# Twelve chunks of the branch gates multiplied inside the attention loop of the first mixer, with their logits kept in DRAM

## What is computed

```python
u = _rmsnorm(h, norm_mix)
(nq, kc, vc, ksl, vsl, kwn, vwn, ng, sq, sk, sv, ga, gb) = jnp.split(u @ w_in, pts, axis=-1)
...
o_a = _nsa(nq, kc, vc, ksl, vsl, kwn, vwn, ng, ...)      # compressed, selected and windowed attention, 8 heads
o_b = _banded_attention(sq, sk, sv, SWA_WINDOW, sinks)   # window of 128 with sinks, 8 heads
merged = jax.nn.sigmoid(ga) * (o_a @ w_branch_a) + jax.nn.sigmoid(gb) * (o_b @ w_branch_b)
h = h + merged @ w_out
```

## Time and profile before

| | |
|---|---|
| median of three runs | 2995.52 us (2992.05 to 3009.61) |
| the profiled execution | 2989.28 us, span 2987.5 us |
| PE, DVE, ACT, POOL busy in the span | 92%, 65%, 35%, 43% |
| mean granted clock of PE | 0.955 of full |
| attention loop | from 541.2 to 697.2 us |
| gate stage, to its last matmul | from 697.2 to 787.8 us |

### The profile page before, as it was taken

One profiled execution on the slowest core, in us unless ns is written; L12 is line 12 of the kernel. 1 busy time (PEld: TensorE's weight loads), 2 busy tenths in 40 slices (PEclk: granted clock), 3 DMA queues, 4 the chain that ended last, 5 costly groups with the idle time before them and its releaser, 6 DMA issues. The chain is left out here.

```text
span 2987.5 us, 38641 instructions
## 1 busy us (share of the span) xinstructions
PE 2740.0 (92%) x14085; PEld 2295.0 (77%) x14085; DVE 1947.1 (65%) x3130; ACT 1037.2 (35%) x1635; POOL 1283.5 (43%) x607
## 2 busy tenths in 40 slices
PE   7998999778989998979988999998999969999996
PEld 5887877336778887758876789998999958888785
DVE  5444232683454444366555267778999969999998
ACT  4232321453233223222022233334655524444342
POOL 3443442002434443423042356773222247777773
PEclk9999999699999999989798999999999989999998
DMA  5443341002234443322002245557999999999993
GB/s 177 136 152 116 106 151 50 1 1 64 91 99 141 150 131 113 99 84 78 15 1 64 83 133 158 165 171 282 344 341 353 343 306 373 376 370 376 377 374 137
DMA packets 186680, 528.83 MB, mean 177 GB/s; under 512 B 14032, under 2 KB 96336, under 8 KB 166480
## 3 DMA queue, kind: packets, MB, share of 16 engines
q1 hardware_dynamic: 80208, 292.66, 30.4%
q0 software_dynamic: 18432, 134.23, 11.5%
q10 hardware_dynamic: 87936, 100.68, 9.8%
HBM read 475.08 MB, written 52.43 MB: 177 GB/s over the span
## 5 line engine op out<-in xcount | busy, mean ns | idle before, releaser
L344 POOL TENSOR_TENSOR ring_low<-ring,ring_high 128x1024 fp32r<-128x1024 f32 x323 | 795.0, 2464 | 1164.4 <-ACT ring_high L311 1164.4
L395 PE MATMUL ps<-u_high,ring_high 128*128 128x512 f32 (+1 forms) x1824 | 695.9, 382 | 44.5 <-DVE u_low L618 17.4
L396 PE MATMUL ps<-u_low,ring_high 128*128 128x512 f32 (+1 forms) x1824 | 686.9, 377 | 0.0
L397 PE MATMUL ps<-u_high,ring_low 128*128 128x512 f32 (+1 forms) x1824 | 686.3, 376 | 0.0
L311 ACT ACTIVATE ring_high<-ring 128x1024 fp32r<-128x1024 f32 x355 | 374.5, 1055 | 618.4 <-PE ps L397 549.4
L395 PEld LDWEIGHTS ps<-u_high,ring_high 128*128 128x128 f32 x1824 | 345.6, 189 | 111.3 <-issue 40.9
L396 PEld LDWEIGHTS ps<-u_low,ring_high 128*128 128x128 f32 x1824 | 346.1, 190 | 52.5 <-issue 2.0
L397 PEld LDWEIGHTS ps<-u_high,ring_low 128*128 128x128 f32 x1824 | 345.7, 190 | 52.6
L2346 POOL DMA_INDIRECT fetched_rows<-in_peer_uv,fetch_index x128 | 165.1, 1290 | 339.7 <-DVE ps L2366 302.4
L344 POOL TENSOR_TENSOR ring_low_more<-ring,ring_high_more 128x1024 fp32r<-128x1024 f32 x96 | 243.2, 2546 | 32.3 <-ACT ring_high_more L311 31.7
L2901 DVE TENSOR_TENSOR expert_coef_low<-expert_product,expert_coef_high 128x384 fp32r<-128x384 f32 x128 | 214.7, 1677 | 0.1
(11 more groups left out here) (427 smaller groups left out, 4863.4 us busy)
## 6 DMA issues: line engine op xcount, KB each, us to landing
ring<-in_peer_u SPq DMA_DIRECT2D x128, 512.0 KB
ring<-in_peer_uv SPq DMA_DIRECT2D x128, 512.0 KB
ring<-in_ffn_gu SPq DMA_DIRECT2D x88, 512.0 KB
ada_weights<-in_ada_w SPq DMA_DIRECT2D x48, 512.0 KB, 3.8
ring<-in_ffn_down SPq DMA_DIRECT2D x48, 512.0 KB
expert_acts<-kept_acts ACTq DMA_DIRECT2D x128, 192.0 KB, 4.0
expert_weights<-weight_stage ACTq DMA_DIRECT2D x24, 1024.0 KB, 8.9
group_acts<-expert_acts ACTq DMA_DIRECT2D x16, 1536.0 KB
```

Of the source, the lines that this page charges most:

```text
L344: pool.tensor_tensor(k.lows[p], k.ring[:, s], k.highs[p].bitcast(F32), ALU.subtract)\
L395: pe.matmul(out, k.highs[p][:, w], high, start=first, stop=False)
L396: pe.matmul(out, k.highs[p][:, w], low, start=False, stop=False)
L397: last = pe.matmul(out, k.lows[p][:, w], high, start=False, stop=final)
```

## The change

Twelve of the sixteen gate chunks are multiplied in the attention loop by the new class `GatesBeside`. Each of the 48 units gets a quarter of a chunk, six matmuls, between score(n+2) and turn(n). The products gather in bank 7, and both kinds of mix now use bank 6. After every fourth unit ACT copies bank 7 into one of two tiles of `rope_pair` and splits the next chunk; SP stores the tile to the DRAM tensor `gate_logits`; POOL makes the low part of a chunk. The gate stage loads the twelve tiles back in three DMAs of 1 MB, multiplies only the last four chunks, and scales and takes the sigmoid of all sixteen. The rounding of `o_t` moves there from DVE to ACT, ahead of the first sigmoid.

```diff
--- before.py
+++ after.py
@@ -44,6 +44,7 @@
 PROJ = 16
+BESIDE = 12
 VEC = {}
@@ -100,9 +101,9 @@
 def heads_of_streams(dram):
-    names = ["ffn1_gu", "ffn1_down", "w_in", "w_in_gates", "w_branch", "w_out", "ffn2_gu", "ffn2_down",
-             "w_in_2_state", "w_in_2", "w_out_2", "peer_wq"]
-    return [[dram[n][j] for j in range(SLOTS)] for n in names] + \
+    names = [("ffn1_gu", 0), ("ffn1_down", 0), ("w_in", 0), ("w_in_gates", 0), ("w_in_gates", BESIDE), ("w_branch", 0),
+             ("w_out", 0), ("ffn2_gu", 0), ("ffn2_down", 0), ("w_in_2_state", 0), ("w_in_2", 0), ("w_out_2", 0), ("peer_wq", 0)]
+    return [[dram[n][at + j] for j in range(SLOTS)] for n, at in names] + \
            [[dram["peer_u"][at + j] for j in range(SLOTS)] for at in (0, P // 2)] + \
@@ -399,6 +400,23 @@
                 after(j)
+    def multiply_part(self, pe, j, lo, hi):
+        k, p = self.k, j % self.parts
+        bank, out, parts, opens, closes, _ = self.chunks[j][1][0]
+        if lo == 0:
+            pe.wait_ge(k.low_ready[p].sem, k.low_ready[p].at(j // self.parts + 1))
+            pe.wait_ge(k.emptied[bank].sem, k.emptied[bank].at(j))
+        for m in range(lo, hi):
+            tile, high, low = parts[m]
+            w = slice(tile * P, (tile + 1) * P)
+            pe.matmul(out, k.highs[p][:, w], high, start=m == 0, stop=False)
+            pe.matmul(out, k.highs[p][:, w], low, start=False, stop=False)
+            last = pe.matmul(out, k.lows[p][:, w], high, start=False, stop=m == len(parts) - 1)
+        if hi == len(parts):
+            last.then_inc(k.used[p].sem, 1)
     def wait_products(self, eng, i, j):
@@ -890,19 +908,26 @@
         shifted.finish()
-def gate_tiles(k, weights, tiles, dst, moving, source, split):
-    stream = plain_stream(k, weights, tiles, 4, KD, moving)
+def gate_tiles(k, weights, dst, moving, beside, source, split):
+    stream = plain_stream(k, weights, SLOTS, SLOTS, KD, moving)
     rounded = k.tiles_rounded
     with ExitStack() as tmp:
         scaled = Signal(tmp, k.nc, "gates_scaled")
+        loaded = [Signal(tmp, k.nc, f"gate_logits_loaded{b}") for b in range(3)]
+        rescaled = Signal(tmp, k.nc, "gate_logits_scaled")
         with k.nc.Block() as block:
             @block.sync
             def _(sp):
+                beside.wait_stored(sp)
+                for b in range(3):
+                    sp.dma_start(dst[:, 4 * b:4 * (b + 1)], k.dram["gate_logits"][4 * b:4 * (b + 1)].rearrange("t p n -> p t n"))\
+                      .then_inc(loaded[b].sem, 16)
                 stream.load(sp)
@@ -916,22 +941,30 @@
                 def epilogue(i, j):
-                    act.wait_ge(scaled.sem, i * 4 + (j + 1))
-                    act.activation(one(dst, i * 4 + j), k.ps[:, j], ACT.Sigmoid).then_inc(k.emptied[j].sem, 1)
+                    if j == 0:
+                        for n in range(KD):
+                            act.activation(split.high[:, n], source[:, n], ACT.Copy).then_inc(rounded.sem, 1)
+                    else:
+                        for n in range(4 * (j - 1), 4 * j):
+                            act.wait_ge(rescaled.sem, n + 1)
+                            act.activation(dst[:, n], dst[:, n], ACT.Sigmoid)
+                    act.wait_ge(scaled.sem, j + 1)
+                    act.activation(dst[:, BESIDE + j], k.ps[:, j], ACT.Sigmoid).then_inc(k.emptied[j].sem, 1)
                 stream.scalar(act, epilogue)
             @block.vector
             def _(dve):
-                for i in range(stream.iters):
-                    for t in range(4):
-                        stream.wait_products(dve, i, t)
-                        dve.tensor_tensor(k.ps[:, t], k.ps[:, t], k.rs[:], ALU.mult).then_inc(scaled.sem, 1)
-                        n = i * 4 + t
-                        if n < KD:
-                            dve.tensor_copy(split.high[:, n], source[:, n]).then_inc(rounded.sem, 1)
-                            dve.wait_ge(rounded.sem, rounded.at(n + 1))
-                            dve.tensor_tensor(split.low[:, n], source[:, n], split.high[:, n].bitcast(F32), ALU.subtract)
+                for n in range(KD):
+                    dve.wait_ge(rounded.sem, rounded.at(n + 1))
+                    dve.tensor_tensor(split.low[:, n], source[:, n], split.high[:, n].bitcast(F32), ALU.subtract)
+                for t in range(4):
+                    stream.wait_products(dve, 0, t)
+                    dve.tensor_tensor(k.ps[:, t], k.ps[:, t], k.rs[:], ALU.mult).then_inc(scaled.sem, 1)
+                    if t < 3:
+                        dve.wait_ge(loaded[t].sem, 16)
+                        for n in range(4 * t, 4 * (t + 1)):
+                            dve.tensor_tensor(dst[:, n], dst[:, n], k.rs[:], ALU.mult).then_inc(rescaled.sem, 1)
     stream.finish()
@@ -1288,7 +1321,62 @@
 KINDS = 3
-def attend(k, c, proj, vtok, sigm, o):
+class GatesBeside:
+    BANK = 7
+    def __init__(self, k, ctx, units):
+        self.k = k
+        self.per = units // BESIDE
+        parts = [(x, k.u.high[:, x], k.u.low[:, x]) for x in range(KD)]
+        self.stream = Stream(k, 1, [(chunk_of(k.dram["w_in_gates"], BESIDE, j),
+                                     [(self.BANK, k.ps[:, self.BANK], parts, True, True, None)]) for j in range(BESIDE)])
+        self.kept = k.pair
+        self.stored = [Signal(ctx, k.nc, f"gate_logits_stored{b}") for b in range(2)]
+    def load(self, sp):
+        k, stream = self.k, self.stream
+        ahead = SLOTS + 1
+        stream.load_chunk(sp, 0, SLOTS, stream.chunks[SLOTS][0](0))
+        for j in range(BESIDE):
+            n = j + ahead
+            if n < BESIDE:
+                stream.load_chunk(sp, 0, n, stream.chunks[n][0](0))
+            elif n < BESIDE + SLOTS:
+                stream.load_chunk(sp, 1, n - BESIDE, stream.then[n - BESIDE])
+            sp.wait_ge(k.emptied[self.BANK].sem, k.emptied[self.BANK].at(j + 1))
+            sp.dma_start(k.dram["gate_logits"][j], self.kept[:, j % 2]).then_inc(self.stored[j % 2].sem, 16)
+    def multiply(self, pe, n):
+        j, part = n // self.per, n % self.per
+        self.stream.multiply_part(pe, j, KD * part // self.per, KD * (part + 1) // self.per)
+    def first_split(self, act):
+        self.stream.split_high(act, 0, 1)
+    def take(self, act, n):
+        if n % self.per or n == 0:
+            return
+        k, j = self.k, n // self.per - 1
+        self.stream.wait_products(act, 0, j)
+        if j >= 2:
+            act.wait_ge(self.stored[j % 2].sem, 16 * (j // 2))
+        act.activation(self.kept[:, j % 2], k.ps[:, self.BANK], ACT.Copy).then_inc(k.emptied[self.BANK].sem, 1)
+        if j + 2 < BESIDE:
+            self.stream.split_high(act, 0, j + 2)
+        elif j + 2 == BESIDE:
+            self.stream.split_high(act, 1, 0)
+    def wait_stored(self, sp):
+        for b in range(2):
+            sp.wait_ge(self.stored[b].sem, 16 * BESIDE // 2)
+def attend(k, c, proj, vtok, sigm, o, ctx):
@@ -1310,7 +1398,8 @@
         mixed = sem("att_mixed")
-        emptied = [sem(f"att_emptied{b}") for b in range(2)]
+        emptied = sem("att_emptied")
+        gates = GatesBeside(k, ctx, len(units))
         def blocks_of(n):
@@ -1348,12 +1437,11 @@
                     first, count = blocks_of(4 * group)
-                    bank, which = (7, 1) if kind == 2 else (6, 0)
                     for g in range(2):
                         pe.wait_ge(copied[g].sem, 4 * group + 4)
-                    if kind != 1 and qt >= 1:
-                        pe.wait_ge(emptied[which].sem, qt)
-                    out = [k.ps[HD * g:HD * (g + 1), bank] for g in range(2)]
+                    if kind == 2 or (kind == 0 and qt >= 1):
+                        pe.wait_ge(emptied.sem, 2 * qt + kind // 2)
+                    out = [k.ps[HD * g:HD * (g + 1), 6] for g in range(2)]
                     if kind == 0:
@@ -1370,6 +1458,7 @@
                         score(n + 2)
+                    gates.multiply(pe, n)
                     turn(n)
@@ -1410,17 +1499,28 @@
                     at = 4 * (kind - 1)
-                    act.activation(o[:, at:at + 4, qt * P:(qt + 1) * P], k.ps[:, 5 + kind].rearrange("p (h q) -> p h q", q=P),
-                                   ACT.Copy).then_inc(emptied[kind - 1].sem, 1)
+                    act.activation(o[:, at:at + 4, qt * P:(qt + 1) * P], k.ps[:, 6].rearrange("p (h q) -> p h q", q=P),
+                                   ACT.Copy).then_inc(emptied.sem, 1)
+                gates.first_split(act)
                 exp(0)
                 for n in range(len(units)):
+                    gates.take(act, n)
                     if n + 1 < len(units):
                         exp(n + 1)
                     copy(n)
                     if n % 4 == 2 and n > 4:
                         empty(n // 4 - 1)
+                gates.take(act, len(units))
                 empty(len(units) // 4 - 1)
+            @block.sync
+            def _(sp):
```

(13 more changed lines are left out.)

## The result

| | before | after |
|---|---|---|
| median of four runs each, on one chip | 2993.78 us (2990.82 to 3009.61) | 2957.66 us (2939.91 to 2963.07) |
| the profiled execution | 2989.28 us | 2956.52 us |
| its span | 2987.5 us | 2954.8 us |

After over before is 0.986, 95% interval 0.982 to 0.991, so the kernel is faster by 0.9 to 1.8%. A second measurement of the same two kernels, in the first experiment, gave 0.9825 (0.9809 to 0.9842). The forecast was 2953 us.

A forecast was written before the change was run, and what follows sets the result against it. PE was to bound the loop in nearly every unit: 167.1 + 7 + 3 + 4 = 181.1 us against 156.0. With the gate stage 64.5 shorter, 2989.3 - 39.4 + 2.8 gave 2953 us, range 2930 to 2988.

The forecast's parts named there:

- the walk: Gate stage followed instruction by instruction from its start: 28 us (25 to 33), with PE standing 4.0 at the third chunk.
- PE's own sum: Attention loop: scores, turns, mixes, compressed part, gate chunks and switches at full clock, 163.4 us, with 3.7 at the ends 167.1.
- change of kind of matmul, a unit: Attention loop: PE's switch to and from gate matmuls costs 0.15 us in each of 48 units, 7.2 (0 to 11.5).
- ACT's splits and copies: Attention loop: ACT's bank 7 copies and chunk splits ahead of exponentials add 0.6 us each, 12 times: 7 (0 to 20).
- lock of POOL and DVE: Attention loop: POOL's 12 subtractions hold DVE instructions, adding 3 us to the path (0 to 24.7).
- clock: Attention loop: the clock rises soon after the loop starts; 4 us counted for the start (0 to 25).
- bank 6 merged: Attention loop: second use of bank 6 by the mixes costs 0, up to 12 x 0.3 us.
- rival 1: Attention loop: PE's switches and ACT's extra work cost nothing, 14 us less, 2939 us; chance 0.12.
- Rival 2: Attention loop: the lock between POOL and DVE reaches the path, 24.7 us instead of 3, 2975 us; chance 0.12.
- Two signs that I named: Attention loop: a maximum over 2 us on the counterpart of L1462, DVE's scaling of probabilities; and DVE's idle time grown.
- Rivals 3 and 4: Loop clock: 3, a third stays at 1.2 GHz, 2974 us, chance 0.10; 4, 1.2 GHz throughout, 3091, chance 0.03.
- Rival 5: Attention loop: all 288 matmuls, switches and ACT's 20 us lie on the path, 92 us longer, 3020 us; chance 0.05.

The follow-up runs named there:

- the first experiment: The changed kernel timed again with no edit, in three rounds: 2940.34 us against 2993.38 before, ratio 0.9825.
- the version with the splits ahead: Changed kernel with ACT, in the gate stage, splitting the third chunk ahead of the first sigmoid and the fourth right behind it: 2938.08 us, gate stage 24.44.
- splits short: Changed kernel with ACT making the high parts of ten chunks in the attention loop for two columns only: 2956.54 us, loop 167.49.
- POOL short: Changed kernel with POOL subtracting only 2 of 1024 columns of the low parts of eleven chunks: 2955.66 us, loop 167.82.
- one bank: Kernel before the change, with all mixes using bank 6 and nothing else changed: 2992.36 us, loop 155.69 against 156.02.

## Why the prediction was right, and where it was off

**Gate stage: right.** 26.6 against 28 forecast, inside 25 to 33; 65.9 us saved against 64.5. The stall at the third chunk is there, 2.3 instead of 4.0. Its chain is that of the walk, but for one step: I had put the table load (1.28) between the first scale and the first sigmoid. It runs at 717.20, ahead of the scale and beside DVE, and costs the path nothing. With DVE's 0.7 us that brings the third chunk's split forward from 11.4 to 9.25; POOL's subtraction of it took 2.95 and not 2.4, which gives some back. DVE's eight subtractions started 1.4 us after the start (713.56 less 712.15) and not at 3.3; only one of them was held by POOL (2487 ns, the median is 680), and they ended at 8.1 and not 8.8. The three loads landed after 5.4 to 9.9 us and nobody waited for one. The order of ACT was the cause of the stall: the version with the splits ahead has none.

**Loop: the mechanism right, the additions too large.** Forecast 181.1, measured 169.3. That is under 172, which I had named as a sign of being wrong, and by that sign this part of the sum was wrong. That PE would be the bound came true (busy 163.4 of 169.3 us). PE's own sum, 163.4 and 3.7 at the ends, was 167.1. The terms on top measured:

| term | taken | measured | by |
|---|---|---|---|
| change of kind of matmul, a unit | 0.15 | 0.13 in the mean of the 48 units | as 678.29 to 679.79 less 6 x 0.227 = 0.14 |
| ACT's splits and copies | 7 | 1.9 for the splits; PE waits 1.8 for the copies | splits short; the group of L414 |
| lock of POOL and DVE | 3 | 1.5 | POOL short |
| clock | 4 | 0 | clock 1.00 in the loop |
| bank 6 merged | 0 | -0.3, within the scatter | one bank |

In the run with the splits short, PE's instructions from start to start are the nearest to what PE needs by itself: scores 33.5, gate matmuls with the change of kind 71.5, transpositions 28.2, mixes 25.1 and the compressed part 4.0, together 162.2. So PE's own sum was at least 1.2 too large, mostly in the transpositions (29.5 taken). With 3.5 of idle time at the ends and 1.8 for the copies that is 167.5, and the loop of after is 1.8 longer. These 1.8 are the cost of the splits. How much of the lock's 1.5 is in them, and how much still in the 28.2, no run tells.

The step that failed is ACT's: I took 0.6 us for each of 12 copies and splits, but ACT waits 62.7 us for turned units in this loop, and most of its two instructions come out of that wait. The step on the clock failed too: I counted 4 us for a slow start, where the first of the gate matmuls already follow each other at the distance of the full clock:

```profile
546.00 0.40 PE L415 MATMUL ps<-u_low,ring_high 128*128 128x512 f32 x1
546.23 0.39 PE L416 MATMUL ps<-u_high,ring_low 128*128 128x512 f32 x1
```


**The whole: two errors of opposite sign, 13 us and about 17.** The two stages gave 52.6 us and not 39.4. Had nothing else moved, the profiled execution would have been near 2938; the second measurement, 2940.34, is that. The first, 2957.66, near my 2953, holds in its profile the 17.4 us of the recurrence at 1.2 GHz, and its four executions fit: 2956.52, 2963.07 and 2958.8 us have a mean clock of 0.953 to 0.955, and 2939.91 us has 0.962. That the forecast was so close to the first measurement is luck: the recurrence stands in none of its reasons. By the stages, rival 1 (switches and ACT cost nothing, 2939) gives the better total, although its first half is wrong: the switches do cost 0.13 each. It is the splits, the lock and the clock that cost little.

**Rival 2, the lock on the path:** its mechanism is real, up to 2.5 us on one instruction, and 28 us in the loop, the clock's part with it, when DVE sets the pace. In the changed kernel it costs 1.5, for the reason that I gave (DVE is no longer the bound), and this is now shown and not only argued. Two signs that I named were wrong. The maximum is not on the scaling but on the small operations (1550 ns). And DVE's idle time did not grow, 33.0 us against 35.2 before: the lock keeps it busy 11.3 us longer.

**Rivals 3 and 4, the clock:** fell for this loop, 1.00. The idle matmuls show that more work for PE is enough to raise it: with 96 full matmuls more, and nothing else changed, the kernel with one bank goes from 0.79 to 1.00. (In rival 4 I took the 2.8 off the 39.4, where it doesn't belong: the time of the kernel before, 2995.5, is 42.5 us above the forecast and not 36.6. Nothing rests on it, as the clock stayed up.) The Trainium skill ("TensorE: Matmul & The Clock Gate", Part 1) says that the gate follows how busy PE is. In the loop the runs agree with it in direction (0.79 to 1.00 with more work). The recurrence does not agree with so simple a reading: PE is busy 20.00 of 20.00 us at 0.50 there in one execution, and at 1.00 with the same instructions in another.

**Rival 5, nothing hidden:** fell. But the run with the matmuls behind the turn shows that place decides how much is hidden: there the loop is 29.5 us longer than before, in front of the turn 13.3.

## What to carry to other kernels

Work moved onto an engine that waits is hidden best where it stands in its queue in front of the instruction that waits; behind it, the same work cost 16 us more here. Where such work goes with a higher granted clock of TensorE, it can shorten the chain by itself (12.6 us with products that nobody reads), so read the clock beside the busy time. A lock or a wait costs what it costs on the engine that sets the pace: eleven subtractions on POOL cost 28 us or 1.5, and only shortening them in both kernels tells which. When a forecast meets the measured time, compare the stages too: here one stage that nobody touched made up 17 us.

## What the runs showed of the hardware that I had not expected

- A DVE operation of two columns takes up to 1550 ns (161 in the median) when it meets a POOL subtraction of 2.4 us, and a `tensor_scalar` 2590 (353).
- The same stage of the same program ran at a granted clock of 0.50 for some 40 us in 3 of 13 profiles, 17.4 us longer, PE busy in both cases.
- Two unread matmuls a unit made the whole kernel shorter: span 2977.3 against 2990.6 us.
